# Scores of the last layer's attention heads: two fp32 matmuls a head become four fp32r matmuls over 128 rows, with the query split on ScalarE and VectorE and part of the softmax weights scaled on ScalarE

## The reference, cut to what matters

```
s_s = einsum('btgrd,bgtkld->bgrtkl', qblk, ksel) * scale + b_s     # selected keys, 64 rows deep
s_w = einsum('bhqd...', qblk, kw) * scale + rel_bias_heads(d_w)    # window keys
p   = softmax(s);  o = g[1] * p_s @ v_s + g[2] * p_w @ v_w
```

## Time and profile before

| | |
|---|---|
| median of 3 runs | 1939.32 us (1939.25 to 1939.57) |
| profiled execution | 1939.51 us, span 1938.1 us |
| mean granted TensorE clock | 1.000 |
| busy: TensorE, its weight loads, VectorE, ScalarE | 100%, 85%, 71%, 51% of the span |
| matmul instructions | 9878 |

### The profile page before, as it was taken

One profiled execution on the slowest core, in us unless ns is written; L12 is line 12 of the kernel. 1 busy time (PEld: TensorE's weight loads), 2 busy tenths in 40 slices (PEclk: granted clock), 3 DMA queues, 4 the chain that ended last, 5 costly groups with the idle time before them and its releaser, 6 DMA issues.

```text
span 1938.1 us, 25274 instructions
## 1 busy us (share of the span) xinstructions
PE 1932.4 (100%) x9878; PEld 1642.0 (85%) x9878; DVE 1379.1 (71%) x2059; ACT 996.6 (51%) x1421; POOL 0.2 (0%) x4
## 2 busy tenths in 40 slices
PE   9999999999999999999999999999999999999999
PEld 7889988988888888898888888888888888888887
DVE  6877778986555687998788887489666444666654
ACT  5545555675556545585566655444444333444442
POOL 0000000000000000000000000000000000000000
PEclk9999999999999999999999999999999999999999
DMA  8454325555544455545534345555555555555563
GB/s 328 172 193 179 131 96 187 177 198 190 193 163 151 176 194 196 196 174 198 217 122 152 113 158 197 199 185 190 185 190 207 199 202 190 192 184 195 186 227 109
DMA packets 51706, 353.20 MB, mean 182 GB/s; under 512 B 5652, under 2 KB 7196, under 8 KB 9860
## 3 DMA queue, kind: packets, MB, share of 16 engines
q1 hardware_dynamic: 50016, 348.84, 50.2%
q10 hardware_dynamic: 1572, 2.75, 0.4%
HBM read 349.47 MB, written 2.11 MB: 181 GB/s over the span
## 4 chain that ended last, share of the span: by engine, by line
PE 93%; DVE 5%; ACT 1%; issue 1%; ACTq 0%; DVEq 0%
PE bank L1236 93%; DVE WL L2171 2%; DVE AR L2361 0%; ACT WH L1663 0%; DVE ft L2954 0%; DVE AR L2474 0%; DVE XP L2357 0%; DVE AR L2471 0%; DVE XP L2459 0%; PE bank L1381 0%; DVE AR L2350 0%; DVE AR L2385 0%; DVE AR L2384 0%; ACT XP L1800 0%; ACT L1676 0%
## 5 line engine op out<-in xcount | busy, mean ns | idle before, releaser
L1663 ACT ACTIVATE WH<-raw 128x1024 fp32r<-128x1024 f32 x649 | 683.7, 1057 | 679.8 <-PE bank L1236 672.1
L2171 DVE TENSOR_TENSOR WL<-raw,WH 128x1024 fp32r<-128x1024 f32 x649 | 783.9, 1222 | 300.9 <-ACT WH L1663 296.9
L1236 PE MATMUL bank<-WH,FP 128*128 128x512 f32 x1408 | 434.5, 389 | 0.1
L1236 PE MATMUL bank<-XP,WH 128*128 128x512 f32 (+2 forms) x1328 | 418.3, 388 | 0.4 <-DVE XP L2459 0.2
L1236 PE MATMUL bank<-WH,XP 128*128 128x512 f32 (+1 forms) x1216 | 379.0, 389 | 0.2 <-DVE WL L2171 0.2
L1236 PEld LDWEIGHTS bank<-WH,FP 128*128 128x128 f32 x1408 | 264.4, 188 | 55.8 <-DVE WL L2171 1.0
L1236 PEld LDWEIGHTS bank<-XP,WL 128*128 128x128 f32 (+1 forms) x1248 | 234.0, 187 | 48.0 <-issue 0.7
L1236 PE MATMUL bank<-WL,FP 128*128 128x512 f32 x704 | 274.0, 389 | 0.0
L1236 PEld LDWEIGHTS bank<-WH,XP 128*128 128x128 f32 x1216 | 226.7, 188 | 44.8 <-DVE WL L2171 0.5
L1236 PE MATMUL bank<-XP,WL 128*128 128x256 f32 (+2 forms) x1248 | 258.3, 279 | 0.1
L1236 PE MATMUL bank<-WL,XP 128*128 128x512 f32 (+1 forms) x608 | 233.5, 384 | 0.0
(11 more groups left out here) (339 smaller groups left out, 1647.4 us busy)
## 6 DMA issues: line engine op xcount, KB each, us to landing
raw<-in_W SPq DMA_DIRECT2D x326, 1024.0 KB, 4.8
out<-XT ACTq DMA_DIRECT2D x8, 256.0 KB, 2.4
raw<-in_W SPq DMA_DIRECT2D x3, 512.0 KB, 6.9
X<-in_x SPq DMA_DIRECT2D x3, 512.0 KB, 12.6
AR<-rv SPq DMA_DIRECT2D x1, 1024.0 KB, 5.9
cst<-in_cst SPq DMA_DIRECT2D x1, 899.5 KB, 11.8
raw<-in_W SPq DMA_DIRECT2D x2, 256.0 KB, 4.4
AR<-in_sgu SPq DMA_DIRECT2D x1, 512.0 KB, 5.9
```

The source lines that it names most:

```text
L1236: return pe.matmul(o, lhsT, rhs, start=start, stop=stop)
L1663: ac.activation(w_slot(WH, s), raw_half(hf), ACT.Copy).then_inc(s_hi, 1)
L2171: tt(w_slot(WL, s), raw_half(pl.half_of[s]), w_slot(WH, s).bitcast(F32), ALU.subtract).then_inc(s_lo, 1)
```

## The change

The scores are computed from two parts of the query and two of the key. For a head the block `QS` (two buffers, by turns) holds the query's high part in the 64 rows of its group and its low part in the other 64. `KH` holds the key's high part in both halves and `KL` its low part. TensorE runs QS against KH and then against KL, so that all four products are summed, in fp32r, for 512 and for 256 columns: four matmuls where there were two.

New steps: "k high" (three ScalarE copies of 64x512), "k low" (three VectorE subtractions of 64x512), "k turn" (three ScalarE copies, which turn to the second group's keys), "q high" (a ScalarE copy of 64x256 per head) and "q low" (a VectorE subtraction of 64x256 per head). In a3 VectorE scales only the two parts of 128x128; "a3 wide" scales the two of 128x256 on ScalarE, as the last step in a pipeline step, and a4 waits for both. The keys' scaling becomes two instructions instead of four, without the zero half.

```diff
     def a0(h):
+        if h == 0:
+            say("q high", 1)
         say("a0", h)
+        if h < 7:
+            say("q low", h + 1)
+        if h == 1:
+            say("k turn")
     def a1(h):
+        if h < 6:
+            say("q high", h + 2)
         say("a1", h)
...
-    p.pipe(8, ["a0", a1, "a2", "a3", "a4", "a5", "a6", a7], wos, 46, (6, 1, 4, 0), (7, 6, 5, 1, 4, 3, 2, 0),
+    p.pipe(8, [a0, a1, "a2", "a3", "a4", "a5", "a6", a7], wos, 46, (6, 1, 4, 0), (7, 6, 5, 1, 4, 3, 2, 0, (3, "a3 wide")),
...
-                    mm(X1[:, 0:512], q[:, 128:256], k, True, True)
-                    mm(Y1[:, 0:256].rearrange("p (s k) -> p s k", s=2), q[:, 0:128],
-                       k.rearrange("p (s k) -> p s k", s=2)[:, :, 0:128], True, True).then_inc(s_n1, 1)
+                    mm(two(X1[:, 0:512]), q[:, 128:256], k, True, False)
+                    mm(two(X1[:, 0:512]), q[:, 128:256], kl, False, True)
+                    mm(two(Y1[:, 0:256]), q[:, 0:128], k[:, :, 0:128], True, False)
+                    mm(two(Y1[:, 0:256]), q[:, 0:128], kl[:, :, 0:128], False, True).then_inc(s_n1, 1)
...
+            def q_high(h):
+                sl = slice(64 * (h // 4), 64 * (h // 4) + 64)
+                if h >= 2:
+                    ac.wait_ge(s_n1, h - 1)
+                ac.activation(QS[h % 2][sl, :], blk(QZ, h % 4)[sl, :], ACT.Copy).then_inc(s_qh, 1)
...
+            def q_low(h):
+                sl, to = slice(64 * (h // 4), 64 * (h // 4) + 64), slice(64 - 64 * (h // 4), 128 - 64 * (h // 4))
+                dv.wait_ge(s_qh, h + 1)
+                tt(QS[h % 2][to, :], blk(QZ, h % 4)[sl, :], QS[h % 2][sl, :].bitcast(F32), ALU.subtract).then_inc(s_kl, 1)
...
+                elif what == "a3 wide":
+                    i = h % 4
+                    ac.wait_ge(s_nw, h + 1)
+                    for s in (0, 1):
+                        ap = seg(h)[s]
+                        ins = ac.activation(ap, ap, ACT.Copy, scale=sm[i][:, s:s + 1])
+                    ins.then_inc(s_n4a, 1)
...
-                    chain(tt(sm[i], sm[i], GX[:, 6 * h:6 * h + 4], ALU.mult))
-                    for s, ap in enumerate(seg(h)):
+                    tt(sm[i], sm[i], GX[:, 6 * h:6 * h + 4], ALU.mult).then_inc(s_nw, 1)
+                    dv.wait_ge(s_nw, h + 1)
+                    for s in (2, 3):
+                        ap = seg(h)[s]
                         ins = ts(ap, ap, sm[i][:, s:s + 1], None, ALU.mult)
                     ins.then_inc(s_n4, 1)
```

More of the change, by code:

```diff
@@ L679, in plan @@
              23: [("qk rstd", 1)], 25: [("qk scaled", 1), ("qk squares", 2)], 27: [("zeros", 2), ("qk rstd", 2)],
-             29: [("qk scaled", 2)]}
+             29: [("qk scaled", 2)], 30: ["k high"]}
     for at in range(31):
@@ L693, in plan @@
     for step in (("nsa gates", 0), ("cmp gelu", 0), ("zeros", 3), ("zeros", 0)):
+        if step[0] == "cmp gelu":
+            say("k low")
         say(*step)
@@ L724, in d5 @@
         say("d5", h)
+        if h == 6:
+            say("q high", 0)
         if h == 7:
             say("sg gelu", 0)
+            say("q low", 0)
     p.pipe(8, ["d0", "d1", "d2", "d3", "d4", d5, "d6"], gating_and_cz(), 38, (0, 3, 5))
@@ L1053, in build @@
         zb = ar(WK + 2048, 960).rearrange("p (l i g n) -> p l i g n", l=16, i=2, g=2)
-        KZ = ar(5120, 544)
-        kswn, kcz = [ar(5120, 512), blk(RAW, 6, 2)], ar(5632, 32)
+        kcz = ar(WK + 5976, 32)
+        KN, KL = blk(RAW, 6, 2), ar_r("KL", 7680, 512)
+        KH = [ar_r(f"KH{g}", 5120 + 512 * g, 512) for g in range(2)]
+        KX = ar_r("KX", WK + 768, 1280)
+        KL1 = bass.AP(KX[:, :].tensor, KX[:, :].offset, [list(KX[:, :].ap[0]), [1024, 2], [1, 256]])
+        QS = [ar_r(f"QS{i}", 13824 + 256 * i, 256) for i in range(2)]
         kcn_, sqk_ = kcn[:, 0:15], sqk[:, 0:15]
@@ L1134, in build @@
         s_e3, s_qk, s_gates = sem("s_e3"), sem("s_qk"), sem("s_gates")
-        s_m0, s_m1, s_m2, s_m4, s_m3, s_m5, s_mnum, s_msq, s_mcap, s_mden, s_mrs = (
-            sem("s_ml_" + n) for n in ("spread", "sc", "dec", "exp", "wt", "pv", "num", "sq", "cap", "den", "rs"))
+        s_m0, s_m1, s_m2, s_m4, s_m3, s_m5, s_mnum, s_msq, s_mden = (
+            sem("s_ml_" + n) for n in ("spread", "sc", "dec", "exp", "wt", "pv", "num", "sq", "den"))
         s_oln, s_oex, s_oh, s_zg, s_ztr, s_zbl, s_zhi, s_zlo = (
@@ L1152, in build @@
         s_cz = sem("s_cz")
+        s_nw, s_n4a = sem("s_at_wt"), sem("s_at_nma")
+        s_kh, s_kl, s_qh = (sem("s_" + n) for n in ("kh", "kl", "qh"))
         s_sgel, s_sgst, s_sgrs, s_sgn, s_sgm, s_sgo = (sem("s_sg_" + n) for n in ("gel", "st", "rs", "nm", "mm", "out"))
@@ L1165, in build @@
         s_dnf = sem("s_dnf")
-        s_tap, s_conv, s_zsl, s_raws, s_us = (sem("s_" + n) for n in ("tap", "conv", "zsl", "raws", "us"))
+        s_tap, s_conv, s_raws, s_us = (sem("s_" + n) for n in ("tap", "conv", "raws", "us"))
         def outed(name, n, half=0):
@@ L1599, in pe_program @@
                     take(4)
[L1600 to L1603, removed]
-                    mm(X1[:, 0:512], q[:, 128:256], k, True, True)
-                    mm(Y1[:, 0:256].rearrange("p (s k) -> p s k", s=2), q[:, 0:128],
-                       k.rearrange("p (s k) -> p s k", s=2)[:, :, 0:128], True, True).then_inc(s_n1, 1)
+                    if h == 4:
+                        pe.wait_ge(s_kh, 6)
+                    pe.wait_ge(s_kl, 3 + h + 1)
+                    q = QS[h % 2]
+                    two = lambda ap: ap.rearrange("p (s k) -> p s k", s=2)
+                    k, kl = two(KH[h // 4][:, :]), two(KL[:, :]) if h < 4 else KL1
+                    mm(two(X1[:, 0:512]), q[:, 128:256], k, True, False)
+                    mm(two(X1[:, 0:512]), q[:, 128:256], kl, False, True)
+                    mm(two(Y1[:, 0:256]), q[:, 0:128], k[:, :, 0:128], True, False)
+                    mm(two(Y1[:, 0:256]), q[:, 0:128], kl[:, :, 0:128], False, True).then_inc(s_n1, 1)
                     free[3] = free[4] = s_n2s, h + 1
@@ L1612, in pe_program @@
                     pe.wait_ge(s_n4, h + 1)
+                    pe.wait_ge(s_n4a, h + 1)
                     for s in range(2):
@@ L1905, in act_program @@
                         ac.wait_ge(s_gates, 5)
-                        ac.activation(den, den, ACT.Exp).then_inc(s_mcap, 1)
+                        ac.activation(den, den, ACT.Exp).then_inc(s_mden, 1)
                     ac.wait_ge(s_m2, h + 1)
@@ L1928, in act_program @@
                 elif what == "cell sums":
-                    ac.wait_ge(s_mden, 1)
+                    ac.wait_ge(s_mden, 2)
                     ac.activation(den, den, ACT.Square, scale=(256 * EPS) ** 0.5).then_inc(s_mden, 1)
-                    ac.wait_ge(s_mden, 3)
-                    rstd(rsh, ssq, 256, 4).then_inc(s_mrs, 1)
+                    ac.wait_ge(s_mden, 4)
+                    rstd(rsh, ssq, 256, 4).then_inc(s_mden, 1)
                 elif what == "o end":
@@ L1999, in act_program @@
                     rstd(rs6, bank[7][:, :], 64, 0).then_inc(s_qrs, 1)
+                elif what == "k high":
+                    ac.wait_ge(s_qsc, 3)
+                    for g, half in ((1, 1), (0, 0), (0, 1)):
+                        ac.activation(KH[g][64 * half:64 * half + 64, :], KN[64 * g:64 * g + 64, :],
+                                      ACT.Copy).then_inc(s_kh, 1)
                 elif what == "cmp gelu":
@@ L2056, in act_program @@
                     ac.activation(lA[h % 4], zA[h % 4], ACT.Exp).then_inc(s_g5e, 1)
+                elif what == "q high":
+                    q_high(n)
                 elif what == "sg gelu":
@@ L2067, in act_program @@
                     b_half(n)
+                elif what == "q high":
+                    q_high(n)
+                elif what == "k turn":
+                    ac.wait_ge(s_g7, 8)
+                    two = lambda ap: ap.rearrange("p (s k) -> p s k", s=2)
+                    for half in range(2):
+                        ac.activation(KL1[64 * half:64 * half + 64], two(KH[1][0:64, :].bitcast(F32)),
+                                      ACT.Copy).then_inc(s_kh, 1)
+                    ac.wait_ge(s_kh, 5)
+                    ac.activation(KH[1][0:64, :], KH[1][64:128, :].bitcast(F32), ACT.Copy).then_inc(s_kh, 1)
                 elif what == "sg gelu":
@@ L2590, in dve_program @@
                     dn = HN.rearrange("p (s v) -> p s v", v=VW)[:, :, T]
-                    dv.wait_ge(s_mcap, 1)
+                    dv.wait_ge(s_mden, 1)
                     dv.wait_ge(s_mnum, 8)
@@ L2594, in dve_program @@
                     stt(den, dn, -1.0, den, ALU.mult, ALU.max).then_inc(s_mden, 1)
-                    dv.wait_ge(s_mden, 2)
+                    dv.wait_ge(s_mden, 3)
                     dv.wait_ge(s_msq, 16)
@@ L2599, in dve_program @@
                     if h == 0:
-                        dv.wait_ge(s_mrs, 1)
+                        dv.wait_ge(s_mden, 5)
```

(16 more changed lines are left out.)

## The result

The changed kernel took 1943.53 us (median of 14 runs, 1943.11 to 1945.45) against 1939.43 us before (14 runs): ratio 1.0024, 95% interval 1.0017 to 1.0031. It is slower by 4.1 us, just beyond what can be told from no change. The forecast was 1942.3 in a range of 1938.7 to 1944.6, with "the same" as the likeliest sign: the mechanism was right, its size some one microsecond short, so that the time lies beyond the 1941.3 to 1943.2 of the forecast proper and in the range of rival D.

The account below looks back on a forecast made before the run. TensorE and VectorE were both taken as full in the 38 us stretch; 4.6 us saved against 7.6 of new TensorE waits made it 2.99 late, 1942.5 from the profiled 1939.51, so 1942.3 as median, range 1938.7 to 1944.6.

Parts of the forecast that it names:

- the same: Whole kernel: a time within about 0.2% of the kernel before, 1935.4 to 1943.2 us; chance 0.61.
- the forecast proper: Whole kernel: 1942.3 us, with 1941.3 to 1943.2 as its own range; chance 0.47.
- rival D: As the forecast with dearer "q low", dearer scaling pairs and late ScalarE weight blocks: 1943.2 to 1944.8 us; chance 0.25.
- The saving: TensorE's a0: shorter matmuls save 0.575 us a head, 4.6 us for eight heads.
- VectorE's first wait: Head 1's "q low" ahead of the norm waits for "q high" behind a ScalarE weight block: VectorE 1.41 us late.
- VectorE's added work: Heads 2 to 6: five "q low" add 1.70 us, three lighter a3 return 1.59; 1.52 late at head 3's product.
- The copy out of bank 7: Head 0's a7 on ScalarE waits behind head 3's scaling pair; TensorE's a6 of head 1 starts 2.21 us late.
- The later copies: ScalarE's scaling pairs delay later a7: TensorE's a6 of heads 2, 3 and 4 start 1.83, 2.60 and 2.99 us late.
- What was hidden: The keys' split, 2.5 us of VectorE within 3.5 idle before 946.73 and copies in 4.2 us of ScalarE, costs nothing.
- Rival B: VectorE's lateness decides, the place of "a3 wide" doesn't: 1939.2 to 1940.3 us; chance 0.2.
- Rival A: The waits don't show and TensorE alone sets the pace: 1934.7 us; chance 0.08.
- The rule of the Trainium skill: In this stretch VectorE (96%), not TensorE (81%), sets the time; a shorter a0 is worth nothing while VectorE is late.

Follow-up runs that it names:

- the first experiment: The changed kernel with VectorE's low part of head 1's query moved ahead of head 0's bias step instead of the spatial gate's norm: 1942.20 us.
- the second experiment: The changed kernel with the wide scaling on ScalarE right behind the following pipeline step's copy out of bank 7, not at its own step's end: 1940.73 us.
- both moves: The changed kernel with head 1's low part ahead of head 0's bias step and the wide scaling behind the copy out of bank 7: 1939.47 us.
- fourth experiments: The changed kernel with all four scalings of the weights on VectorE, as in the kernel before, and none on ScalarE: 1941.88 us.
- the low part done twice: Both moves plus bias step and gate product ahead of VectorE's projection tiles, with the low-part subtraction done twice per head from the second on: 1941.11 us.
- a lighter one: Both moves plus bias step and gate product ahead of VectorE's projection tiles, with all four scalings of a head on ScalarE: 1940.08 us.
- the fastest run: Both moves, bias step and gate product ahead of VectorE's projection tiles, wide scaling behind ScalarE's weight block and copies of banks 5 and 6: 1937.44 us.
- the last experiment: The fastest run with VectorE's bias step and gate product ahead of everything else in the pipeline step, "q high" at the front too: 1941.00 us.

## Why the prediction was right, and where it was short

- **The saving.** 1.285 to 0.71 us a head was forecast; the four matmuls of head 0 take 0.69, from 1033.07 to the tile behind them:

```profile
1033.07 0.39 PE L1256 MATMUL bank<-KH,QS 128*128 128x512 f32 x1
...
1033.76 0.40 PE L1256 MATMUL bank<-XP,WH 128*128 128x512 f32 x1
```

  Right.
- **VectorE's first wait.** 1.41 us late at the norm: 1.40 measured. The wait and its cause were right, and the first experiment took it away; that the number fits to 0.01 us is in part luck. The section began 0.14 us earlier than before, which hides the 0.11 that "q low" took beyond its 0.34. And the start that it counts from, 1034.58, was set by a DMA: in the runs with nothing ahead of the norm it starts between 1033.72 and 1034.41.
- **VectorE's added work: the term that was mis-sized.** I took 0.34 us to the next start for "q low", from a neighbour of 128 rows, and kept 0.42 as the upper end. It took 0.45: 

```profile
1055.63 0.48 DVE L2977 TENSOR_SCALAR AR<-AR,small 128x128 f32<-128x128 f32 x2
1056.15 0.42 DVE L2811 TENSOR_TENSOR QS<-AR,QS 64x256 fp32r<-64x256 f32 x1
1056.60 1.23 DVE L2226 TENSOR_TENSOR WL<-raw,WH 128x1024 fp32r<-128x1024 f32 x1
```

  And where it follows the narrow scalings these take 0.52 to its start instead of 0.40, so that a3 gives back 0.41 there, not 0.53. At head 3's product: 1.41 + 5 x 0.45 - (0.41 + 0.53 + 0.41) = 2.31; measured 1073.70 - 1071.38 = 2.32, forecast 1.52. This 0.8 is most of the 1.1 that the sum was short. The hand-over that I took as 0.15 us worked the other way: TensorE starts 0.10 behind VectorE's L2964 (1053.02, then 1053.12) and 0.05 behind L2168 (1075.07, then 1075.12).
- **The copy out of bank 7.** The mechanism and its place were right: 1.54 us of TensorE behind L2168, and the second experiment removed it. a6 of head 1 starts 0.73 later than forecast, by the term above.
- **What was left out.** The forecast let TensorE wait for L2899 at the scores of head 6 (0.99 us late; measured 1.75) and had no wait at those of head 3, where it stood 1.54 us. In the changed kernel this adds nothing to the end as far as the timelines show, since VectorE has no idle time there and TensorE stands again before a6 of head 1; with that wait gone it is the largest that is left (1.57 us with both moves).
- **The later copies.** From a6 of head 1 to a6 of head 4 the forecast had +0.78 us, measured 0.94 (2.94 to 3.88). Right.
- **What was hidden.** The keys' split cost nothing: TensorE waits nowhere between 900 and 1022 us, and VectorE kept 1.04 us idle before the copy that stood behind 3.51.
- **Rival D**, the dear pieces, is where the time lies, and of its pieces the first is what happened: "q low" cost more than I took. The pair of scalings didn't (0.81 to the next start, 1073.90 to 1074.71), and late weight blocks did not come. Its pieces add up to 1943.0 to 1943.8, not to the 1944.8 that it names. **Rival B** fell with the second and fourth experiments. **Rival A** needed four changes of order to be approached: 1937.4 against its 1934.7.
- **VectorE as the bound.** The rule of the Trainium skill, "Perfetto Trace Analysis", section "Identifying the Most-Contended Engine", which takes the engine of highest occupancy as the one to work on, agrees with the low part done twice: 1.67 us of 1.8 reached TensorE at head 4. It doesn't agree with the runs that moved scalings: a heavier VectorE was faster by 1.2 us, a lighter one, with ScalarE heavier, slower by 1.0, and the fastest run has VectorE's load unchanged at 36.57 us. (Each of these differences is smaller than 1.7 us; TensorE's waits in the traces bear them out.) What remains open: how far below 1937.4 a full search over the orders of both lists would come.

## What to carry to other kernels

When one engine's time is cut, look in the other engines' lists for what stands ahead of the instructions that release it; a short piece of new work that waits there for a late result costs its wait, not its duration. Before moving work to an engine that is free half the time, look up what was ready behind the place where it is put in. Cost a small new instruction by rows with its own shape and rows of partitions, and by the time from start to start, not by its neighbour.

## What the runs showed of the hardware that I had not expected

"q low" reads 64 rows and writes the other 64. It doesn't overlap with its neighbours on VectorE: 0.45 us from its start to the next, and 0.12 us more behind the narrow scalings ahead of it, where a multiplication of 128x256 in place (L2870) leaves 0.34. The crossing isn't needed for that. In the kernel before, L2820 copies 64x256 out of a bank to the same rows, rows 0 to 63 for an even head and 64 to 127 for an odd one; heads 6 and 7, each with the same operation behind it:

```profile
1018.86 0.42 DVE L2820 COPY AR<-bank 64x256 f32<-64x256 f32 x1 [0.55 <-PE bank L1236]
1019.20 2.34 DVE L2171 TENSOR_TENSOR WL<-raw,WH 128x1024 fp32r<-128x1024 f32 x2
...
1027.47 0.43 DVE L2820 COPY AR<-bank 64x256 f32<-64x256 f32 x1
1027.93 1.23 DVE L2171 TENSOR_TENSOR WL<-raw,WH 128x1024 fp32r<-128x1024 f32 x1
```

0.34 us to the next start for rows 0 to 63, 0.46 for rows 64 to 127; heads 0 and 1 show the same, 0.33 and 0.46 (from 990.48 and 995.32). An output in fp32r isn't the reason either: L2886 writes 128x256 of it and leaves 0.34 (1090.38, then 1090.72). These rows were in the trace of the kernel before, and would have given the term as 0.45.

In the last experiment TensorE's granted clock fell after it had stood for 3.52 us; waits of up to 1.7 us in this section in the other runs left it at 1.00. The windows of 2 us there (columns as above):

```profile
1038.00:1040.00 2.00, 0.00 (x0) 0.00 (x0) 2.00 (x4) 0.84 (x2) 0.00 (x0) 0.92 0.01 4
1040.00:1042.00 2.00, 1.74 (x5) 1.50 (x5) 1.97 (x4) 0.00 (x0) 0.00 (x0) 0.50 0.00 0
1042.00:1044.00 2.00, 2.00 (x10) 1.69 (x10) 1.56 (x5) 0.00 (x0) 0.00 (x0) 0.73 0.00 0
1044.00:1046.00 2.00, 2.00 (x13) 1.77 (x12) 1.94 (x4) 1.16 (x2) 0.00 (x0) 1.00 0.26 37
```

It is 0.50, the lower of its two levels (1.2 of 2.4 GHz), from 1040 on, and back at 1.00 by 1044. Against the run that it comes from, at full clock, the same matmuls are 3.70 us later where TensorE starts again and 5.07 us later 2.7 us on: the clock cost some 1.4 us beside the wait.
